# Moving two post-norm seams into PSUM and scoring the matrix memory in row pairs

## What is computed

```python
def first_block(x, ...):
    hn = rms_norm(x, norm_mix_pre)
    mix = hybrid_mixer(hn, ...)                  # matrix memory (mLSTM) heads and gated linear attention heads
    x = x + rms_norm(mix, norm_mix_post)         # seam 1: the norm behind the mixer
    hn = rms_norm(x, norm_ffn_pre)
    ff = conv_ffn(hn, ...)
    x = x + rms_norm(ff, norm_ffn_post)          # seam 2: the norm behind the feed-forward
    return x
# rms_norm(y, g) = y * rsqrt(mean(y*y, axis=-1) + EPS) * g
# matrix memory: 4 heads, keys of width 64; scores s = q k^T over all 512 x 512 pairs, then decay weights
```

## Time and profile before

| | |
|---|---|
| runs shown | 2164.86 us median of 3 (2164.64 to 2168.41) |
| the profiled execution | 2168.39 us, its span 2166.6 us |
| PE busy | 2059.2 us, 95% of the span |
| DVE, ACT, POOL busy | 1066.1, 584.2 and 1465.8 us |
| TensorE clock, mean of the span | 0.974 of full |
| chain that ended last | PE 83%, DVE 11%, ACT 2%, issue 2%, POOL 1% |

### The profile page before, as it was taken

The page is one execution under the profiler, slowest core; times in us unless marked ns, Lnnn a source line. Parts: engine busy times, 40 slices in busy tenths (PEclk is TensorE's granted clock), DMA queues, the critical chain, the costliest instruction groups (busy, mean ns, idle before and its releaser), DMA issues.

```text
span 2166.6 us, 25549 instructions
## 1 busy us (share of the span) xinstructions
PE 2059.2 (95%) x9398; PEld 1647.8 (76%) x9398; DVE 1066.1 (49%) x1575; ACT 584.2 (27%) x1097; POOL 1465.8 (68%) x723
## 2 busy tenths in 40 slices
PE   7998898999999799789999999999999999999997
PEld 5767676888888678667688888877768768888886
DVE  4347736423434799873553232373466355323234
ACT  4236443221111324321221010124662122101011
POOL 6413346877777677665487877776667548787774
PEclk9999998999999899989999999999999999999999
DMA  4102123323232234322132322222102213232221
GB/s 175 59 30 69 40 89 101 107 97 97 90 97 91 76 125 155 98 78 78 40 106 88 107 97 96 88 93 83 59 11 88 78 45 101 88 107 98 97 85 61
DMA packets 55464, 187.75 MB, mean 87 GB/s; under 512 B 6080, under 2 KB 7872, under 8 KB 55264
## 3 DMA queue, kind: packets, MB, share of 16 engines
q1 hardware_dynamic: 50976, 179.07, 24.9%
q10 hardware_dynamic: 4384, 7.21, 1.0%
HBM read 183.37 MB, written 2.10 MB: 86 GB/s over the span
## 4 chain that ended last, share of the span: by engine, by line
PE 83%; DVE 11%; ACT 2%; issue 2%; POOL 1%; DMA 0%; SPq 0%; DVEq 0%; POOLq 0%; ACTq 0%
PE bank L568 25%; PE bank L569 24%; PE bank L570 24%; DVE bank L2181 3%; PE bank L930 2%; PE bank L1146 1%; PE bank L773 1%; PE bank L1160 1%; PE bank L1176 1%; DVE qkL L2061 1%; POOL wH L514 1%; PE bank L725 1%; DVE MIX L1879 1%; PE bank L855 1%; PE bank L622 1%
## 5 line engine op out<-in xcount | busy, mean ns | idle before, releaser
L514 POOL TENSOR_TENSOR wH<-raw,zero 128x1024 fp32r<-128x1024 f32 (+2 forms) x309 | 596.0, 1929 | 515.4 <-PE bank L570 507.7
L517 POOL TENSOR_TENSOR wL<-raw,wH 128x1024 fp32r<-128x1024 f32 (+2 forms) x309 | 738.2, 2389 | 24.3
L568 PE MATMUL bank<-hnH,wH 128*128 128x512 f32 (+1 forms) x1472 | 584.9, 397 | 39.6 <-DVE hnL L1794 31.4
L569 PE MATMUL bank<-hnL,wH 128*128 128x512 f32 (+1 forms) x1472 | 578.0, 393 | 0.0
L570 PE MATMUL bank<-hnH,wL 128*128 128x512 f32 (+1 forms) x1472 | 577.6, 392 | 0.0
L568 PEld LDWEIGHTS bank<-hnH,wH 128*128 128x128 f32 (+1 forms) x1472 | 277.2, 188 | 111.0 <-DVE hnL L1794 37.8
L570 PEld LDWEIGHTS bank<-hnH,wL 128*128 128x128 f32 (+1 forms) x1472 | 277.1, 188 | 61.7 <-issue 0.8
L569 PEld LDWEIGHTS bank<-hnL,wH 128*128 128x128 f32 (+1 forms) x1472 | 277.3, 188 | 61.2 <-issue 2.2
L568 PE MATMUL bank<-actH,wH 128*128 128x512 f32 x784 | 308.8, 394 | 4.2 <-DVE actL L2236 4.2
L570 PE MATMUL bank<-actH,wL 128*128 128x512 f32 x784 | 306.0, 390 | 0.0
L569 PE MATMUL bank<-actL,wH 128*128 128x512 f32 x752 | 293.5, 390 | 0.0
(11 more groups left out here) (330 smaller groups left out, 2513.9 us busy)
## 6 DMA issues: line engine op xcount, KB each, us to landing
raw<-weights SPq DMA_DIRECT2D x315, 512.0 KB, 3.5
raw<-weights SPq DMA_DIRECT2D x28, 384.0 KB, 2.9
XT<-x_t SPq DMA_DIRECT2D x8, 256.0 KB, 6.8
XT<-x_t ACTq DMA_DIRECT2D x1, 2048.0 KB, 8.3
out<-MIX ACTq DMA_DIRECT2D x8, 256.0 KB, 2.2
memT<-mem_t ACTq DMA_DIRECT2D x1, 1024.0 KB, 5.4
KC<-KC ACTq DMA_DIRECT2D x3, 256.0 KB, 3.9
CT<-consts ACTq DMA_DIRECT2D x1, 552.0 KB, 5.7
```

Of the source, the lines that this page charges most:

```text
L514: nc.gpsimd.tensor_tensor(wH[:, slot, 0:w], raw[:, slot, 0:w], nothing.broadcast_to([P, w]), ALU.add)\
L517: nc.gpsimd.tensor_tensor(wL[:, slot, 0:w], raw[:, slot, 0:w], wH[:, slot, 0:w].bitcast(F32), ALU.subtract).then_inc(split, 1)
L568: mm(out_, aH, bH, start=first, stop=False)
L569: mm(out_, aH, bL, start=False, stop=False)
```

## The change

**Scores.** SP copies queries and keys to the other half of the partitions: four DMAs of 256 KB, `qkA` to a new `qkO` (which shares its place with `VB`, written later), between the loads of `a_v` and of `b_qk`, once ACT has evacuated all four `a_qk` tiles. `score_tiles` then takes two key blocks at a time, the second from `qkO`, so from the other half of the rows.

**Seams.** The squares of w_out's and `ff0_d2`'s tiles are made in the tile's own bank, and DVE adds them from there (`post_squares`). Ln and Exp of the post-norm stay in the row sum's bank. In `post_norm` the scaled chunk and the new x are made in one of two banks (`fresh_bank`); ACT makes `high` from there and copies the new x back to XT, and `low` reads the bank as well. The sum of the new x's squares stays as it was (ACT to MIX, eight adds of DVE in SBUF). The row sum of seam 2 moves from behind the second memory unit to behind the first, and from bank 0 to bank 7.

```diff
+            def exchange():
+                for i in range(4):
+                    gone_wait(sp, TILE0["a_qk"] + i)
+                for pair in range(2):
+                    for half in range(2):
+                        sp.dma_start(qkO[64 - 64 * half:P - 64 * half, pair, :, :],
+                                     qkA[64 * half:64 * half + 64, pair::2, :]).then_inc(sig("exchanged"), 16)
...
+                if u0 == POS["b_qk", 0]:
+                    exchange()
...
             def score_tiles(h):
-                for j in range(NB):
+                other = slice(64 - 64 * (h % 2), P - 64 * (h % 2))
+                pe.wait_ge(sig("exchanged"), 16 * 4)
+                for j in range(0, NB, 2):
                     n = TILE0[f"s{h}"] + j
                     claim(n)
+                    claim(n + 1)
                     mm(psum(n)[:, :], qkA[rows, 2 + h // 2, j * P:j * P + P], qkA[rows, h // 2, :], start=True,
                        stop=True).then_inc(tile_done, 1)
+                    mm(psum(n + 1)[:, :], qkO[other, h // 2, 1, j * P + P:j * P + 2 * P], qkO[other, h // 2, 0, :],
+                       start=True, stop=True).then_inc(tile_done, 1)
...
-            for i in (0, 1):
-                memory_key(i)
-            row_sums(TILE0["post1"], "post1")
-            for i in (2, 3):
+            memory_key(0)
+            post_sums("post1")
+            for i in (1, 2, 3):
                 memory_key(i)
...
-            def post_chunk(c_):
-                square(MIX[:, c_, :])
+            def post_chunk(n, m):
+                run(MIX[:, m, :], psum(n)[:, :], ACT.Copy).then_inc(sig("post_copied"), 1)
+                run(psum(n)[:, :], psum(n)[:, :], ACT.Square).then_inc(sig("post_sq"), 1)
+            def post_norm(post, next_norm):
...
+                for c_ in range(KD):
+                    act.wait_ge(sig("x_new"), first + c_ + 1)
+                    fresh = fresh_bank(post, c_)
+                    high(hnH[:, c_, :], fresh, v(next_norm, c_))
+                    run(XT[:, c_, :], fresh, ACT.Copy).then_inc(sig("x_copied_back"), 1)
+                    if c_ > 0:
+                        new_square(c_ - 1)
...
+                        if f == 0 and t == 2:
+                            tt(psum(n)[:, :], psum(n)[:, :], acc[:, m, :], ALU.add).then_inc(sig("post_sum"), 1)
+                            if m > 0:
+                                post_squares("ff0_d2", m - 1)
+                            continue
...
                 for c_ in range(KD):
-                    if c_ < KD - 1:
-                        scale(c_ + 1)
-                    stt(XT[:, c_, :], MIX[:, c_, :], v(gain, c_), XT[:, c_, :], ALU.mult, ALU.add)\
-                        .then_inc(sig("x_new"), 1)
+                    fresh = fresh_bank(post, c_)
+                    dve.wait_ge(sig("post_copied"), first + c_ + 1)
+                    if c_ > 1:
+                        dve.wait_ge(hn_ready, nhn[0])
+                    tt(fresh, MIX[:, c_, :], root, ALU.mult).then_inc(sig("post_scaled"), 1)
+                    dve.wait_ge(sig("post_scaled"), first + c_ + 1)
+                    stt(fresh, fresh, v(gain, c_), XT[:, c_, :], ALU.mult, ALU.add).then_inc(sig("x_new"), 1)
                     if c_ > 0:
-                        low(hnL[:, c_ - 1, :], XT[:, c_ - 1, :], v(next_norm, c_ - 1), hnH[:, c_ - 1, :])
+                        new_low(c_ - 1)
```

More of the change, by code:

```diff
@@ L239 @@
 ROWS_AT = (0, 512, 1024, 896)
+POSTS = {"post0": ("w_out", (("norm_b", 2), ("w_out", 6))), "post1": ("ff0_d2", (("ff0_d2", 2), ("ff0_d2", 5)))}
 def key_tile(i):
@@ L1479, in _, with new_square @@
             head_high(3)
-            def post_chunk(c_):
-                square(MIX[:, c_, :])
+            def post_chunk(n, m):
+                run(MIX[:, m, :], psum(n)[:, :], ACT.Copy).then_inc(sig("post_copied"), 1)
+                run(psum(n)[:, :], psum(n)[:, :], ACT.Square).then_inc(sig("post_sq"), 1)
+            def post_norm(post, next_norm):
+                n, first = TILE0[post], KD * list(POSTS).index(post)
+                nc.scalar.preload_act_table_set("natural_log_exp_and_others")
+                tile_wait(act, n)
+                free(run(psum(n)[:, :], psum(n)[:, :], ACT.Ln, bias=v("eps"), scale=1.0 / D), n)
+                gone_wait(act, n)
+                run(psum(n)[:, :], psum(n)[:, :], ACT.Exp, scale=-0.5).then_inc(rstd_ready, 1)
+                def new_square(c_):
+                    act.wait_ge(sig("x_copied_back"), first + c_ + 1)
+                    square(XT[:, c_, :], dst=MIX[:, c_, :])
+                for c_ in range(KD):
[5 more added lines that the diff above has]
+                        new_square(c_ - 1)
+                new_square(KD - 1)
             for m in range(KD):
@@ L1485, in _ @@
                 tile_wait(act, n)
[L1486 to L1493, removed]
+                post_chunk(n, m)
+            post_norm("post0", "ffn_pre")
             act.dma_start(memT[:, :, :], mem_t.rearrange("(k p) m -> p k m", p=P)).then_inc(mem_in, 16)
@@ L1498, in _ @@
             for m in range(KD):
[L1499 to L1505, removed]
+                act.wait_ge(sig("post_sum"), m + 1)
+                post_chunk(TILE0["ff0_d2"] + m, m)
+            post_norm("post1", "mix2_0")
             row_root(TILE0["row_sum3"])
@@ new lines, in feed_forward, with post_squares @@
+                if f == 0:
+                    post_squares("ff0_d2", KD - 1)
+                else:
+                    norm_chunk(next_norm, KD - 1)
+            def post_squares(name, m):
+                n = TILE0[name] + m
+                posts[0] += 1
+                dve.wait_ge(sig("post_sq"), posts[0])
+                if m == 0:
+                    free(nc.vector.tensor_copy(ssq[:, :], psum(n)[:, :]), n)
+                else:
+                    free(tt(ssq[:, :], psum(n)[:, :], ssq[:, :], ALU.add), n)
+                gone_wait(dve, n)
@@ new lines, in post_norm, with new_low @@
+            def post_norm(post, gain, next_norm):
+                first = KD * list(POSTS).index(post)
+                root = psum(TILE0[post])[:, :]
+                root_wait()
+                for name, m in POSTS[post][1]:
+                    gone_wait(dve, TILE0[name] + m)
+                def new_low(c_):
+                    dve.wait_ge(sig("x_copied_back"), first + c_ + 1)
+                    low(hnL[:, c_, :], fresh_bank(post, c_), v(next_norm, c_), hnH[:, c_, :])
+                for c_ in range(KD):
+                    fresh = fresh_bank(post, c_)
[5 more added lines that the diff above has]
+                    stt(fresh, fresh, v(gain, c_), XT[:, c_, :], ALU.mult, ALU.add).then_inc(sig("x_new"), 1)
```

41 lines of the change are left out of this document (19 added, 22 removed).

## The result

| | before | after |
|---|---|---|
| median of the runs | 2166.64 us (4 runs, 2164.64 to 2170.06) | 2150.02 us (4 runs, 2149.39 to 2152.27) |
| ratio, 95% interval | | 0.9924, 0.9906 to 0.9941 |
| profiled execution, span | 2168.39 us, 2166.6 us | 2152.27 us, 2150.5 us |
| PE, DVE, ACT, POOL busy | 2059.2, 1066.1, 584.2, 1465.8 us | 2054.9, 1037.8, 593.8, 1457.8 us |

What follows compares the result with a forecast made beforehand. PE was taken as the bound, busy 2059.2 of 2166.6 us. Scores 7.1, seam 1 3.3 and seam 2 10.6 sum to 21.0 us: 2147.4 for the profiled execution, 2143.9 against the median; range 2137 to 2153.

Steps and rivals of the forecast that it cites:

- Scores, 7.1: Attention scores: two row halves work at once, a head's records take 1.92 us, 1.78 less; 7.1 us over four heads.
- The rival with partial overlap: Scores: the second of a pair starts half a step (0.22 us) late, 1.8 us less gain, 2145.7; chance 0.05.
- The exchange, 0: DMAs ahead of the scores: cost nothing, hidden by the projection `a_v`; up to 16 us without that cover.
- Seam 1, 3.3: From w_out's last tile: PE restarts at 336.1 instead of 340.61, row sum ends the stretch 3.3 us earlier.
- seam 1's squares all meet POOL: Seam 1: a chunk over 2.3 us instead of 2.2, seam loses 4.3 instead of gaining 3.3: 2151.5; chance 0.12.
- Seam 2, 10.6: Behind `ff0_d2`'s last tile: DVE no longer late, weights late next; row sum at 744.2 instead of 754.82, 10.6 us.
- DVE held with one SBUF operand: Seams: one SBUF operand is held too, or PSUM operands cost more; seam 2 keeps only 2.8 us: 2151.7; chance 0.03.
- The round trip (slower): Seam chunks: `low` waits for ACT's copy, 3.64 us a chunk if nothing overlapped, 5.7 slower, 2170.6; chance 0.03.
- The clock: PE's half clock, as near 140 us: shorter scores may spare such a stretch or bring one, 3 us either way.

Runs made afterwards that it cites:

- The parts: Kernel before with exchange and score pairs alone: 6.5 us less, ratio 0.9971; changed kernel with scores as before and no exchange: 12.8 us less, ratio 0.994.
- the two kernels with the squares in the bank: Changed kernel with the new squares added up in the root's bank, 2149.42 us; the same with the post-norms' root in SBUF, 2151.76 us.

## Why the prediction was right, and where it was off

The time lay in the range, and the mechanism was the one forecast; 2149.7 us is the median of all 13 runs of the changed kernel, 5.8 over the forecast. Two things make up that distance. (By its own terms the low end of the range is 2164.86 - 27.0 = 2137.9, not 2137.)

**The reference (4.1 us).** The forecast set its sum against the median of three runs, 2164.86. Over the 66 runs of the kernel before in all groups the median is 2168.98 (2164.64 to 2172.64). The step that failed is "against that median the forecast is 2143.9": with the 3.5 us between profiled run and median in plain sight, that choice moved the forecast by more than any rival in PSUM. Against the profiled execution it was 2147.4. The gain over all runs is 2168.98 - 2149.67 = 19.3 us, for 21.0 forecast. The parts also add up to 19.3 (6.5 + 12.8), but that they agree to a tenth is chance: the changed kernel beside them gained 21.1, and the three comparisons of the changed kernel give 16.6, 21.1 and 18.0 us. What is left of the forecast's distance is within that spread.

**The terms (1.7 us, as sized from profiles).**
- *Scores, 7.1:* 1.99 us a head instead of 1.92, since the first record of a head takes 0.69 us; by the trace 4 x 1.71 = 6.8, by time 6.5 with whatever half clock moved. The pairs overlap fully. The rival with partial overlap, near which the packing figure of the Trainium skill lies (TensorE: Matmul & The Clock Gate, "Part 3: Packing small matmuls"), doesn't hold for two halves here: 3.70 to 1.99 is 1.86x.
- *The exchange, 0:* right, 0.9994. POOL waited 7.8 us in its shade.
- *Seam 1, 3.3:* the root 4.4 us behind ACT's start and the restart at 8.05 (forecast 8.0) are right; the chunks come every 2.24 us (forecast 2.2). From ACT's start to the next row sum it took 33.6 us in the first profile, against 32.9 forecast and 36.2 before: 2.6 us of gain; in the two other profiles of the changed kernel 32.6, 3.6 of gain. The number of squares that meet POOL was right in the first profile (three), but it isn't a constant: with one fewer, as in the two others, PE doesn't wait; with one more it waits 3.7 us, and the stretch takes 36.3 us, no gain at all. The rival "seam 1's squares all meet POOL" was the right mechanism with the wrong trigger; it needs no slower chunk; in the profile that shows it, half clock began a row sum earlier.
- *Seam 2, 10.6:* 51.57 us from last tile to row sum became 41.41, 10.2 of gain. Waits for `wL`, POOL's 4.33 us a unit and the third `pc_in` unit at +18.6 are as forecast.
- *DVE held with one SBUF operand:* falls, 0.68 to 0.76 us for every such instruction of the chunks under POOL. The Trainium skill's advice to copy matmul output to SBUF first where many operations follow (VectorE: DVE Perf Modes, "Rules for kernel authors") would have cost time here, as far as the root shows it: read from SBUF, it lengthened seam 2 by 2.2 us and seam 1 by 0.5 (profiles of the two kernels with the squares in the bank). Their times, 2151.76 and 2149.42, are of different groups and against their own before lie only 0.5 us apart.
- *The round trip (slower):* falls, 2.24 us a chunk against the 3.5 at which it would decide.
- *The clock:* 3 us either way was the right size, but it was put down to the shorter scores alone. The stretch near 140 went, also in the profile with the exchange alone; one near 212 came with the pairs; and the largest piece, at 15 us, has nothing to do with the change.

## What to carry to other kernels

Put one input of a DVE instruction in PSUM where POOL works at the same time: the instruction then costs the same as in quiet, and POOL keeps its pace. When the engine that was late is cured, look at once for the next in line and give it less: here one more step, ACT making `wH` of four units for POOL, shortened PE's wait at seam 2 by 2.1 us and brought about 5 us more by the medians, part of it half clock that fell well. And take the reference of a forecast from many runs, or from the profiled execution whose rows make the sum; before reading 2 or 3 us as an effect, compare a kernel with itself.

## What had not been expected

- A DVE instruction with two SBUF inputs doesn't cost 2.4 us under POOL as such, but its 0.7 and the rest of POOL's instruction: 0.75 to 1.60 us, 1.07 on the mean, when bank work lies between, and POOL pays 0.7 us a unit.
- One addition more that meets POOL decides over some 5 us at and behind seam 1: for kernels that are alike there, the stretch from w_out's last tile to the row sum took 32.6, 33.6 or 36.3 us, and half clock behind the longest wait added about 1.7.
- The kernel before itself spreads over 8 us from run to run, 2164.64 to 2172.64; one piece of it is whether PE is back at full clock at 15 us. Other pieces weren't followed.
